# Rotary embedding on a Trainium2 core: block-exchanging copies in place of rotation products

## The chip, the cores and the metric

The kernel runs on one core of one Trainium2 chip. The metric is the device time of one execution in microseconds (us); three runs of the kernel before gave 915.8, 915.88 and 916.42, median 915.88. Engines are named as the profile names them: PE is TensorE (PEld its weight loads), DVE is VectorE, ACT is ScalarE, POOL is GpSimd, SP the queue that issues most of the loads.

## The reference, cut to what matters

Two transformer blocks run one after the other on 256 tokens of width 1024, in float32. The first has dilated attention, an RWKV-7 time mix and gates; the second three other attentions, gates, a memory and a feed-forward part. In both, queries and keys are rotated by position before they are used; both blocks' functions do the same:

```
half = HEAD_DIM // 2                       # heads of 64 columns
ang = pos[:, None] * inv_freq[None, :]
c, s = jnp.cos(ang), jnp.sin(ang)
x1, x2 = xf[..., :half], xf[..., half:]
return jnp.concatenate([x1 * c - x2 * s, x2 * c + x1 * s], axis=-1)
```

So a row of the first 32 of a head needs its partner 32 rows on, with a minus; a row of the second 32 its partner 32 rows back, with a plus.

## The kernel before, in words

Queries and keys are kept with features on the partitions and the 256 tokens in the free dimension, so a tile of 128 partitions holds two heads, each of two blocks of 32 rows. A projection is done in chunks of 256 features (`feature_chunk`): 8 slices of the model width, each as a product of the high part of the weights, one of their remainder (lines 807 and 808), and one of the high part with the activations' remainder (line 816), for two halves of 128 features, into one PSUM bank. The banks 0 and 1 take turns. The high part of a chunk's weights is copied by ScalarE (`split`, line 1820, in two halves), and VectorE subtracts it from the weights for the remainder (`split`, line 2703, in two halves); chunk n+1's split is done while TensorE works on chunk n, and TensorE's first products of a chunk wait for the first half's remainder.

Block one (tag "qk") has six chunks of first-block queries and keys, n = 0 to 5. Block two (tag "in2") has seven, of which n = 2 to 6 are rotated; n = 6 is 128 features wide, so its bank holds 256 columns and not 512. Behind it come two slots of value weights (464 columns wide), then the gates' slots (512 wide).

The steps of one rotated chunk before the change:

- ScalarE copies the bank to SBUF (`rope_read`, line 1985, recorded at the helper's line 1820) and so frees it in block two.
- TensorE multiplies the copy by a constant 128x128 matrix of ones and minus ones (`rotate`, line 766), in the middle of the next chunk's first half, into a bank of its own.
- The cosine product (copy or bank times cosine): in block one by VectorE from the chunk's bank (`cosines`, line 2809), after ScalarE's copy; in block two by GpSimd from the copy (`rope`, line 3698).
- The sine product by VectorE from the rotation's bank (line 2776).
- The sum of both: in block one by VectorE (line 2815), in block two by GpSimd (line 3703).

The order on each engine is written out by hand: each engine's program is a set of generators that are advanced in the same turns, and each engine takes its instructions strictly in that order. In block one the chunks ("m" turns) run beside the RWKV inverse ("s" turns; lines 1132, 1145, 1158, 1192 to 1225 on TensorE, lines 2957 to 2995 on VectorE, more copies at line 1820 on ScalarE); each of five levels of the inverse shares the time with one chunk. The inverse's banks (4 to 7) go round, and a product waits until the bank's last content was read: the one at line 1145 needs the banks of two transposed tiles (line 727), which ScalarE copies out. In block two ScalarE also makes three small copies of key rows (64x256) behind the last chunk.

Of the kernel before, what the change touches and what calls it, by code (L numbers as in the profile page):

```python
# [21 lines left out]

C_ID, C_SU, C_IU, C_LI, C_ONE, C_BLK, C_ROT, C_M0, C_D64 = [128 * i for i in range(9)]
C_LV = 128 * 9
C_MA = C_LV + 768
# [19 lines left out]
def shape_constants():  # L45
# [40 lines left out]
    c[0:64, C_SINC:C_SINC + 256] = np.tile(sin, (2, 1))  # L86
    return c
# [189 lines left out]
def program(nc, A, consts, vecs, pt, out):  # L277
    with ExitStack() as ctx:
# [55 lines left out]
        def const(off, n):  # L334
            return low[:, OC + off:OC + off + n]
# [236 lines left out]
        main_pe, main_act, main_dve, main_pool = [count("main_" + n) for n in ("pe", "act", "dve", "pool")]  # L572
        rope_pe, rope_act, rope_dve, rope_pool = [count("rope_" + n) for n in ("pe", "act", "dve", "pool")]
        rw_pe, rw_act, rw_dve, rw_pool = [count("rwkv_" + n) for n in ("pe", "act", "dve", "pool")]
# [133 lines left out]
        def tensor_program(e, turns):  # L708
# [42 lines left out]
            def seam(tag, i, at_once=False):  # L751
# [246 lines left out]
            def qkv():  # L998
                for s in range(3, 7):
                    yield from feature_chunk(st1, s, next(pg), plan_z[s][1], z_read(s), nothing)  # L1000
                yield from token_range(st1, V_AT, 2, 512, lambda i: [main_act.at("v", 0, i)], nothing)
                yield from token_range(st1, V_AT + 2, 1, 256, lambda i: [main_act.at("v", 1, i)], nothing)
                for n in range(6):
                    yield from feature_chunk(st1, QK_AT + n, next(pg), [128, 128], [rope_dve.at("qk", n, "cos")],
                                             (lambda n=n: rotate("qk", n - 1, 2, rz1[(n - 1) % 2])) if n else nothing)

# [3 lines left out]
            def gates():  # L1010
                for r in (2, 3, 0, 1):
                    yield from gate(r, (lambda: rotate("qk", 5, 2, rz1[1])) if r == 2 else nothing)

# [444 lines left out]

            def rotate2(n):
                if n >= 2:  # L1460
                    m = 1 if n == 6 else 2
                    rotate("in2", n, m, rz2[n % 2][:, 0:m, :])

            def read2(n):
                return [main_act.at("qa", n) if n < 2 else rope_act.at("in2", n)]

            turns.beside(head("in2", (0, 2), read2, lambda n: rotate2(n - 1)), seam("in2", 1, True), 3)

            def main_b():
                for n in range(2, 7):  # L1470
                    yield from feature_chunk(st2, n - 2, next(pg), plan_2[n][1], read2(n), lambda n=n: rotate2(n - 1))
                yield from token_range(st2, 5, 2, 464, lambda i: [main_act.at("vt2", i), main_dve.at("vt2", i)], lambda: rotate2(6))

# [333 lines left out]
        def scalar_program(e, turns):  # L1807
# [806 lines left out]
        def vector_program(e, turns):  # L2614
# [191 lines left out]

            def cosines(n, b):
                q.wait_ge(*rope_act.at("qk", n))
                tt(rt1[n % 2], halves(bank(b)), rep(const(C_COS, 256), 2), ALU.mult).then_inc(rope_dve.up("qk", n, "cos"), 1)

            def rotate1(n):
                dst = qk[:, 2 * n:2 * n + 2, :]
                rotate("qk", n, 2, dst, const(C_SIN, 256))
                q.wait_ge(*rope_dve.at("qk", n))
                tt(dst, dst, rt1[n % 2], ALU.add).then_inc(rope_dve.up("qk", n, "sum"), 1)

            def qkv():
# [5 lines left out]
                for n in range(6):  # L2823
                    b = next(pg)
                    yield from feature_chunk(st1, QK_AT + n, [128, 128], lambda: cosines(n, b), (lambda n=n: rotate1(n - 1)) if n else nothing)

# [463 lines left out]
            def rotate2(n):  # L3290
                if n >= 2:
                    rotate("in2", n, 1 if n == 6 else 2, rope_to(n), const(C_SINC if n == 6 else C_SIN, 256))

# [16 lines left out]
            def main_b():  # L3310
                for n in range(2, 7):
                    next(pg)
                    yield from feature_chunk(st2, n - 2, plan_2[n][1], nothing, lambda: rotate2(n - 1))
                yield from token_range(st2, 5, 2, read_vt, lambda: rotate2(6))
# [343 lines left out]
        def gpsimd_program(e, turns):  # L3658
# [36 lines left out]

            def rope(tag, n, m, zs, t1, cos):
                q.wait_ge(*rope_act.at(tag, n))
                tt(t1, zs, rep(cos, m), ALU.mult).then_inc(rope_pool.up(tag, n, "cos"), 1)

            def rotate(tag, n, dst, t1):  # L3700
                q.wait_ge(*rope_dve.at(tag, n))
                q.wait_ge(*rope_pool.at(tag, n, "cos"))
                tt(dst, dst, t1, ALU.add).then_inc(rope_pool.up(tag, n), 1)
# [121 lines left out]

            def first2(n):
                if n >= 2:
                    m = 1 if n == 6 else 2
                    rope("in2", n, m, rz2[n % 2][:, 0:m, :], rt2[n % 2][:, 0:m, :], const(C_COSC if n == 6 else C_COS, 256))
# [5 lines left out]
            turns.beside(head("in2", st2, first2, lambda n: second2(n - 1)), seam("in2", 1, True), 3)  # L3835

            def main_b():
                for n in range(2, 7):
                    yield from feature_chunk(st2, n - 2, plan_2[n][1], lambda: first2(n), lambda: second2(n - 1))
                yield from token_range(st2, 5, 2, lambda: second2(6))  # L3840
# [144 lines left out]
```

## Time and profile before

| | |
|---|---|
| three runs | 915.8, 915.88, 916.42 us |
| span of the profiled execution | 913.6 us |
| the runs' median beyond that span | 2.3 us (915.88 - 913.6) |
| TensorE busy | 892.5 us, 98% |
| VectorE busy | 606.5 us, 66% |
| ScalarE busy | 454.0 us, 50% |
| GpSimd busy | 43.3 us, 5% |
| the chain that ended last | TensorE 86%, VectorE 7%, ScalarE 3% |

The profile is of one execution; its page gives the span from the first to the last instruction and no time of its own beside it, so the runs' median is set against the span. A busy share counts an instruction from its start to its end, and neighbours on one engine overlap: where the text speaks of what an instruction costs, it uses the distance from one start to the next. In a timeline, an entry "x4" is four neighbours of one kind, and a bracket is the idle time before an instruction and what ended it.

### The profile page before, as it was taken

How to read it: one execution, taken by the hardware profiler on the slowest of the kernel's cores; microseconds unless marked ns; L12 is line 12 of the kernel's file. 1: busy time of each engine (PE TensorE's matmuls, PEld its weight loads, DVE VectorE, ACT ScalarE, POOL GpSimd, SP SyncE). 2: the span in 40 equal slices, each digit the busy share in tenths (PEclk: the TensorE clock that was granted, in tenths of full speed). 3: DMA queues.
4: the chain of work that ended last, by engine and by line, in shares of the span. 5: the costliest groups of instructions: out<-in, count | busy, mean ns of one | idle time of the engine just before them, and what ended most of it. 6: DMA issues, size and time to landing. Idle time of an engine off the chain costs nothing.

```text
span 913.6 us, 15401 instructions
## 1 busy us (share of the span) xinstructions
PE 892.5 (98%) x6552; PEld 753.8 (83%) x6552; DVE 606.5 (66%) x972; ACT 454.0 (50%) x731; POOL 43.3 (5%) x61
## 2 busy tenths in 40 slices
PE   7999999999899999999999999999999999999997
PEld 4999898787689888888889878776788788888885
DVE  4578978557856666656765577877863566666673
ACT  4775444436534444446444357473522545555561
POOL 0010000010000000000000440000000000000000
PEclk9999999999999999999999999999999999999999
DMA  9644333224578665555439664252717566665621
GB/s 338 187 139 139 102 102 116 60 91 137 187 252 280 187 189 194 202 192 185 135 96 237 151 230 142 94 185 96 263 55 208 138 185 186 191 192 194 201 96 47
DMA packets 131205, 150.78 MB, mean 165 GB/s; under 512 B 11808, under 2 KB 102176, under 8 KB 131008
## 3 DMA queue, kind: packets, MB, share of 16 engines
q1 hardware_dynamic: 129920, 145.57, 51.5%
q10 hardware_dynamic: 1216, 4.23, 1.2%
q8 instruction: 52, 0.85, 0.4%
q14 instruction: 17, 0.14, 0.1%
HBM read 148.73 MB, written 1.05 MB: 164 GB/s over the span
## 4 chain that ended last, share of the span: by engine, by line
PE 86%; DVE 7%; ACT 3%; issue 2%; DMA 1%; POOL 0%; POOLq 0%; ACTq 0%; DVEq 0%
PE psum L834 12%; PE psum L721 9%; PE psum L723 9%; PE psum L722 9%; PE psum L839 7%; PE psum L787 4%; PE psum L807 3%; PE psum L808 3%; PE psum L816 3%; PE psum L727 3%; PE psum L883 2%; PE psum L893 2%; PE psum L884 2%; DVE parts L2703 2%; PE psum L840 2%
## 5 line engine op out<-in xcount | busy, mean ns | idle before, releaser
L1820 ACT ACTIVATE parts<-low 128x1024 fp32r<-128x1024 f32 (+3 forms) x252 | 254.2, 1044 | 68.4 <-PE psum L723 50.2
L2703 DVE TENSOR_TENSOR parts<-low,parts 128x1024 fp32r<-128x1024 f32 (+3 forms) x156 | 186.9, 1228 | 28.5 <-ACT parts L1820 28.3
L721 PE MATMUL psum<-parts 128*128 128x512 f32 (+2 forms) x424 | 170.0, 401 | 1.8 <-DVE parts L2703 1.0
L723 PE MATMUL psum<-parts 128*128 128x512 f32 (+2 forms) x424 | 163.5, 386 | 0.0
L722 PE MATMUL psum<-parts 128*128 128x512 f32 (+2 forms) x424 | 163.4, 385 | 0.0
L1820 ACT ACTIVATE high<-psum 128x512 f32<-128x512 f32 (+4 forms) x95 | 52.4, 563 | 160.7 <-PE psum L840 76.4
L834 PE MATMUL psum<-parts 128*128 128x512 f32 x462 | 116.8, 392 | 0.0
L834 PEld LDWEIGHTS psum<-parts 128*128 128x128 f32 x462 | 86.9, 188 | 16.9
L721 PEld LDWEIGHTS psum<-parts 128*128 128x128 f32 x424 | 79.6, 188 | 23.1 <-issue 3.8
L723 PEld LDWEIGHTS psum<-parts 128*128 128x128 f32 x424 | 79.6, 188 | 16.3
L722 PEld LDWEIGHTS psum<-parts 128*128 128x128 f32 x424 | 79.8, 188 | 14.7 <-issue 0.7
L2768 DVE TENSOR_TENSOR parts<-low,parts 128x1024 fp32r<-128x1024 f32 x54 | 66.0, 1223 | 35.3 <-ACT parts L1820 35.3
L807 PE MATMUL psum<-parts 128*128 128x256 f32 (+2 forms) x312 | 82.4, 300 | 0.0
L808 PE MATMUL psum<-parts 128*128 128x256 f32 (+2 forms) x312 | 76.8, 282 | 0.0
L839 PEld LDWEIGHTS psum<-parts 128*128 128x128 f32 x528 | 72.0, 190 | 5.2
L839 PE MATMUL psum<-parts 128*128 128x256 f32 x528 | 73.6, 282 | 0.0
L807 PEld LDWEIGHTS psum<-parts 128*128 128x128 f32 (+2 forms) x312 | 58.8, 189 | 4.1 <-issue 3.2
L808 PEld LDWEIGHTS psum<-parts 128*128 128x128 f32 (+2 forms) x312 | 58.9, 189 | 2.3 <-issue 2.2
L3199 DVE TENSOR_TENSOR mid<-psum,high 128x512 f32<-128x512 f32 x33 | 22.8, 692 | 46.2 <-ACT high L1820 46.2
L816 PE MATMUL psum<-parts 128*128 128x256 f32 (+2 forms) x312 | 43.7, 283 | 0.0
L3666 POOL TENSOR_TENSOR low<-low 128x1 f32<-128x1 f32 x20 | 11.0, 550 | 635.6 <-DVE low L2624 319.4
L816 PEld LDWEIGHTS psum<-parts 128*128 128x128 f32 (+2 forms) x312 | 40.0, 189 | 0.1
(321 smaller groups left out, 1346.7 us busy)
## 6 DMA issues: line engine op xcount, KB each, us to landing
low<-in_w_in_dram SPq DMA_DIRECT2D x40, 1024.0 KB, 5.3
low<-in_w_ffn_in_dram SPq DMA_DIRECT2D x44, 512.0 KB, 5.2
low<-in_w_ff_in_dram SPq DMA_DIRECT2D x16, 1024.0 KB, 6.1
low<-in_w_ff_out_dram SPq DMA_DIRECT2D x16, 1024.0 KB, 4.9
low<-in_w_ffn_out_dram SPq DMA_DIRECT2D x11, 1024.0 KB, 5.0
low<-in_w_out_dram SPq DMA_DIRECT2D x8, 1024.0 KB, 5.2
low<-in_w_ple_gate_dram SPq DMA_DIRECT2D x4, 1024.0 KB, 5.2
low<-consts_dram ACTq DMA_DIRECT2D x1, 2142.0 KB, 9.2
```

The costliest lines, as they stand in the source:

```text
L721: mm(o, l[0], r[0], start, False)
L722: mm(o, l[0], r[1], False, False)
L723: return mm(o, l[1], r[0], False, stop)
L787: t = mm(PSUM[0:m, banks[n], 256 * j + 128 * i:256 * j + 128 * i + 128], w3[:, k, off:off + m], uT[:, k, 128 * i:128 * i + 128], k == 0, k ...
L807: mm(o, hi[:, k, c], st.uh[:, k, :], k == 0, False)
L808: mm(o, lo_[:, k, c], st.uh[:, k, :], False, False)
L816: t = mm(o, hi[:, k, c], st.ul[:, k, :], False, k == 7)
L834: mm(p, hi[:, k, c], st.u2(k), k == 0, False)
L839: mm(p[:, 0:256], lo_[:, k, c], st.uh[:, k, :], False, False)
L1820: return e.activation(o, a, ACT.Copy)
L2703: tt(rslot3(n, nk, width)[:, r, 0:w], slot3(n, nk, width)[:, r, 0:w], st.hi3(j)[:, r, 0:w].bitcast(F32), ALU.subtract) \
L2768: tt(rview(OR + 2048 * n + 1024 * (k % 2), 1024), slot(n)[:, 1024 * (k % 2):1024 * (k % 2) + 1024], rview(base, 1024).bitcast(F32), ALU.su ...
```

## The change

The rotation product is gone from TensorE, and its constant with it. ScalarE's one copy of a bank becomes four, each of 32 rows, each to the place of its neighbour block, so that the copy holds every row's partner. The minus stands in the table of sines now. The cosine product is VectorE's in both blocks, reads the bank, and comes first: ScalarE's copies wait for it. VectorE's sine product reads the exchanged copy in SBUF. A bank is free when ScalarE's copies are done. GpSimd keeps the sums of block two.

```diff
-    same = r // 64 == s // 64
-    c[:, C_ROT:C_ROT + 128] = (same & (r % 64 < 32) & (s % 64 == r % 64 + 32)) * 1.0 \
-        - (same & (r % 64 >= 32) & (s % 64 == r % 64 - 32)) * 1.0
...
-    c[:, C_SIN:C_SIN + 256] = np.tile(sin, (4, 1))
+    c[:, C_SIN:C_SIN + 256] = np.tile(np.concatenate([-sin, sin]), (2, 1))
...
-            def rotate(tag, n, m, z):
-
-                b = 2 + n % 2 if tag == "qk" else 5 + n % 3
-                p = bank(b)
-                q.wait_ge(*rope_act.at(tag, n))
-                mm(p[:, 0:256 * m], const(C_ROT, 128), z, True, True).then_inc(rope_pe.up(tag, n), 1)
-                free[b] = [rope_dve.at(tag, n)]
...
             def rope_read(tag, n, m, b, zs):
+
                 if n >= (2 if tag == "qk" else 4):
-                    q.wait_ge(*(rope_pe.at(tag, n - 2) if tag == "qk" else rope_pool.at(tag, n - 2)))
-                copy(zs, halves(bank(b))[:, 0:m, :]).then_inc(rope_act.up(tag, n), 1)
+                    q.wait_ge(*rope_dve.at(tag, n - 2))
+                q.wait_ge(*rope_dve.at(tag, n, "cos"))
+                z = halves(bank(b))
+                for p in range(4):
+                    t = copy(zs[32 * p:32 * p + 32, 0:m, :], z[32 * (p ^ 1):32 * (p ^ 1) + 32, 0:m, :])
+                t.then_inc(rope_act.up(tag, n), 1)
...
-            def rotate(tag, n, m, dst, sin):
-                q.wait_ge(*rope_pe.at(tag, n))
-                tt(dst, halves(bank(2 + n % 2 if tag == "qk" else 5 + n % 3))[:, 0:m, :], rep(sin, m), ALU.mult).then_inc(rope_dve.up(tag, n), 1)
+            def cosines(tag, n, m, b, t1, cos, made):
+                q.wait_ge(*made)
+                tt(t1, halves(bank(b))[:, 0:m, :], rep(cos, m), ALU.mult).then_inc(rope_dve.up(tag, n, "cos"), 1)
+
+            def rotate(tag, n, m, zs, dst, sin):
+
+                q.wait_ge(*rope_act.at(tag, n))
+                tt(dst, zs, rep(sin, m), ALU.mult).then_inc(rope_dve.up(tag, n), 1)
...
+            def cosines2(n, b):
+                m = 1 if n == 6 else 2
+                if n >= 4:
+                    q.wait_ge(*rope_pool.at("in2", n - 2))
+                cosines("in2", n, m, b, rt2[n % 2][:, 0:m, :], const(C_COSC if n == 6 else C_COS, 256), main_pe.at("st2", n - 2, 1))
...
-            def rope(tag, n, m, zs, t1, cos):
-                q.wait_ge(*rope_act.at(tag, n))
-                tt(t1, zs, rep(cos, m), ALU.mult).then_inc(rope_pool.up(tag, n, "cos"), 1)
```

How the instructions stand, with what each waits for. First ScalarE in block one, around the reads of chunks 0 and 1, before:

```order
L1820 ACTIVATE mid<-psum 128x512 [waits main_pe]
L1820 ACTIVATE parts<-low 128x1024 [waits slot_in0]
L1820 ACTIVATE high<-psum 128x512 [waits rwkv_pe,z_dve]
L1820 ACTIVATE parts<-low 128x1024
L1820 ACTIVATE high<-psum 128x512 [waits rwkv_pe]
L1820 ACTIVATE mid<-psum 128x512 [waits main_pe]
```

and now:

```order
L1803 ACTIVATE mid<-psum 32x512 [waits rope_dve,main_pe]
L1803 ACTIVATE mid<-psum 32x512 x3
L1803 ACTIVATE parts<-low 128x1024 [waits slot_in0]
L1803 ACTIVATE high<-psum 128x512 [waits rwkv_pe,z_dve]
L1803 ACTIVATE parts<-low 128x1024
L1803 ACTIVATE high<-psum 128x512 [waits rwkv_pe]
L1803 ACTIVATE mid<-psum 32x512 [waits rope_dve,main_pe]
L1803 ACTIVATE mid<-psum 32x512 x3
```

The places are the same; the read is four instructions (to "mid", the copy), and the first of them waits for VectorE's cosine product. The "high" copies are those of the two transposed tiles.

VectorE in block one at the same place, before:

```order
L2964 TENSOR_TENSOR high<-high,low 64x512
L2809 TENSOR_TENSOR mid<-psum,low 128x512 [waits rope_act]
L2776 TENSOR_TENSOR mid<-psum,low 128x512 [waits rope_pe]
L2815 TENSOR_TENSOR mid<-mid 128x512 [waits rope_dve]
L2703 TENSOR_TENSOR parts<-low,parts 128x1024 [waits split_act] x2
```

and now:

```order
L2955 TENSOR_TENSOR high<-high,low 64x512
L2764 TENSOR_TENSOR mid<-psum,low 128x512 [waits main_pe]
L2769 TENSOR_TENSOR mid<-mid,low 128x512 [waits rope_act]
L2804 TENSOR_TENSOR mid<-mid 128x512 [waits rope_dve]
L2691 TENSOR_TENSOR parts<-low,parts 128x1024 [waits split_act] x2
```

No instruction has moved; the cosine product (first of the three) waits for TensorE alone, and the sine product for ScalarE's copies.

VectorE in block two, chunks 2 to 4, before:

```order
L2703 TENSOR_TENSOR parts<-low,parts 128x1024 [waits split_act] x2
L2776 TENSOR_TENSOR high<-psum,low 128x512 [waits rope_pe]
...
L2703 TENSOR_TENSOR parts<-low,parts 128x4x128 [waits split_act] x2
L2776 TENSOR_TENSOR high<-psum,low 128x2x256 [waits rope_pe]
L2703 TENSOR_TENSOR parts<-low,parts 128x928 [waits split_act] x2
```

and now:

```order
L2691 TENSOR_TENSOR parts<-low,parts 128x1024 [waits split_act] x2
L2764 TENSOR_TENSOR high<-psum,low 128x512 [waits main_pe,rope_pool]
L2769 TENSOR_TENSOR high<-high,low 128x512 [waits rope_act]
L2691 TENSOR_TENSOR parts<-low,parts 128x4x128 [waits split_act] x2
L2764 TENSOR_TENSOR high<-psum,low 128x512 [waits main_pe,rope_pool]
L2769 TENSOR_TENSOR high<-high,low 128x2x256 [waits rope_act]
L2691 TENSOR_TENSOR parts<-low,parts 128x928 [waits split_act] x2
```

Between the two remainders of the next weights and the sine product stands a cosine product now, of the chunk that TensorE has just ended.

## Rows read from the trace of the kernel before

**Rows 1.** The page, busy time of each engine and instructions.
```profile
PE 892.5 (98%) x6552; PEld 753.8 (83%) x6552; DVE 606.5 (66%) x972; ACT 454.0 (50%) x731; POOL 43.3 (5%) x61
```

**Rows 2.** Line 766, the rotations: count, duration in ns, first and last start.
```profile
L766 PE MATMUL psum<-mid,low x12: 590/590/594, 94.2 to 147.9; 128*128 128x512 f32 x12
...
L766 PE MATMUL psum<-high,low x10: 378/590/594, 502.4 to 526.7; 128*128 128x512 f32 x8, 128*128 128x256 f32 x2
```

**Rows 3.** TensorE's timeline in block one: start, duration, what, idle before.
```profile
94.24 1.02 PE L766 MATMUL psum<-mid,low 128*128 128x512 f32 x2
95.10 0.60 PE L727 MATMUL psum<-low,high 128*128 128x128 f32 x4
...
101.46 1.16 PE L1145 MATMUL psum<-high 64*128 64x128 f32 x16
...
107.80 0.24 PE L1217 MATMUL psum<-mid,high 64*64 64x64 f32 x1 [0.16 <-DVE high L2971]
```

**Rows 4.** VectorE's timeline in block one.
```profile
90.54 0.45 DVE L2957 COPY_PREDICATED high<-low,psum 128x256 f32<-128x256 int32 x1 [0.98 <-PE psum L1132]
...
98.69 0.69 DVE L2809 TENSOR_TENSOR mid<-psum,low 128x512 f32<-128x512 f32 x1
99.30 0.68 DVE L2776 TENSOR_TENSOR mid<-psum,low 128x512 f32<-128x512 f32 x1
100.02 0.69 DVE L2815 TENSOR_TENSOR mid<-mid 128x512 f32<-128x512 f32 x1
...
118.70 2.35 DVE L2703 TENSOR_TENSOR parts<-low,parts 128x1024 fp32r<-128x1024 f32 x2
123.85 0.69 DVE L2809 TENSOR_TENSOR mid<-psum,low 128x512 f32<-128x512 f32 x1 [2.80 <-ACT mid L1820]
```

**Rows 5.** ScalarE's timeline in block one.
```profile
93.00 0.60 ACT L1820 ACTIVATE mid<-psum 128x512 f32<-128x512 f32 x1 [4.53 <-PE psum L816]
...
112.06 0.60 ACT L1820 ACTIVATE mid<-psum 128x512 f32<-128x512 f32 x1 [1.97 <-PE psum L816]
112.56 2.00 ACT L1820 ACTIVATE parts<-low 128x1024 fp32r<-128x1024 f32 x2
...
123.22 0.60 ACT L1820 ACTIVATE mid<-psum 128x512 f32<-128x512 f32 x1 [1.92 <-PE psum L816]
```

**Rows 6.** ScalarE's timeline in block two.
```profile
501.19 0.60 ACT L1820 ACTIVATE high<-psum 128x512 f32<-128x512 f32 x1 [3.27 <-PE psum L816]
...
507.81 0.60 ACT L1820 ACTIVATE high<-psum 128x512 f32<-128x512 f32 x1 [1.51 <-PE psum L816]
...
524.74 0.38 ACT L1820 ACTIVATE high<-psum 128x256 f32<-128x256 f32 x1 [1.39 <-PE psum L816]
526.22 1.30 ACT L1820 ACTIVATE high<-high 64x256 f32<-64x256 f32 x3 [1.09 <-POOL high L3703]
```

**Rows 7.** TensorE's timeline behind block two's chunks.
```profile
525.10 0.47 PE L721 MATMUL psum<-parts 128*128 128x464 f32 x1 [0.39 <-DVE parts L2703]
...
535.97 0.37 PE L723 MATMUL psum<-parts 128*128 128x464 f32 x1
536.18 0.40 PE L721 MATMUL psum<-parts 128*128 128x512 f32 x1
```

**Rows 8.** ScalarE's timeline behind block one: copies of 64 rows.
```profile
152.73 0.59 ACT L1820 ACTIVATE high<-psum 64x512 f32<-64x512 f32 x1
153.23 0.58 ACT L1820 ACTIVATE mid<-psum 64x512 f32<-64x512 f32 x1
153.83 0.59 ACT L1820 ACTIVATE high<-psum 64x512 f32<-64x512 f32 x1
```

**Rows 9.** GpSimd's and VectorE's timelines in block two.
```profile
504.27 1.30 POOL L3703 TENSOR_TENSOR high<-high 128x512 f32<-128x512 f32 x1 [1.11 <-DVE high L2776]
510.88 2.21 POOL L3703 TENSOR_TENSOR high<-high 128x512 f32<-128x512 f32 x1 [1.11 <-DVE high L2776]
...
511.85 2.32 DVE L2703 TENSOR_TENSOR parts<-low,parts 128x1024 fp32r<-128x1024 f32 x1
```

More of the change, by code:

```diff
@@ L20 @@
 S0 = math.exp(-0.5)
-C_ID, C_SU, C_IU, C_LI, C_ONE, C_BLK, C_ROT, C_M0, C_D64 = [128 * i for i in range(9)]
-C_LV = 128 * 9
+C_ID, C_SU, C_IU, C_LI, C_ONE, C_BLK, C_M0, C_D64 = [128 * i for i in range(8)]
+C_LV = 128 * 8
 C_MA = C_LV + 768
@@ L572, in program @@
         main_pe, main_act, main_dve, main_pool = [count("main_" + n) for n in ("pe", "act", "dve", "pool")]
-        rope_pe, rope_act, rope_dve, rope_pool = [count("rope_" + n) for n in ("pe", "act", "dve", "pool")]
+        rope_act, rope_dve, rope_pool = [count("rope_" + n) for n in ("act", "dve", "pool")]
         rw_pe, rw_act, rw_dve, rw_pool = [count("rwkv_" + n) for n in ("pe", "act", "dve", "pool")]
@@ L1003, in qkv @@
                 for n in range(6):
-                    yield from feature_chunk(st1, QK_AT + n, next(pg), [128, 128], [rope_dve.at("qk", n, "cos")],
-                                             (lambda n=n: rotate("qk", n - 1, 2, rz1[(n - 1) % 2])) if n else nothing)
+                    yield from feature_chunk(st1, QK_AT + n, next(pg), [128, 128], [rope_act.at("qk", n)], nothing)
             def gate(r, late):
@@ L1011, in gates @@
                 for r in (2, 3, 0, 1):
-                    yield from gate(r, (lambda: rotate("qk", 5, 2, rz1[1])) if r == 2 else nothing)
+                    yield from gate(r, nothing)
             rw_bank = itertools.cycle((4, 5, 6, 7))
@@ L1457, in tensor_program @@
             st2 = ST["st2"]
[L1459 to L1462, printed above, removed]
             def read2(n):
                 return [main_act.at("qa", n) if n < 2 else rope_act.at("in2", n)]
-            turns.beside(head("in2", (0, 2), read2, lambda n: rotate2(n - 1)), seam("in2", 1, True), 3)
+            turns.beside(head("in2", (0, 2), read2, nothing), seam("in2", 1, True), 3)
             def main_b():
                 for n in range(2, 7):
-                    yield from feature_chunk(st2, n - 2, next(pg), plan_2[n][1], read2(n), lambda n=n: rotate2(n - 1))
-                yield from token_range(st2, 5, 2, 464, lambda i: [main_act.at("vt2", i), main_dve.at("vt2", i)], lambda: rotate2(6))
+                    yield from feature_chunk(st2, n - 2, next(pg), plan_2[n][1], read2(n), nothing)
+                yield from token_range(st2, 5, 2, 464, lambda i: [main_act.at("vt2", i), main_dve.at("vt2", i)], nothing)
             turns.alone(main_b())
@@ L2804, in vector_program @@
             e.tensor_copy(identb, ident).then_inc(init_dve.up("idb"), 1)
-            def cosines(n, b):
-                q.wait_ge(*rope_act.at("qk", n))
-                tt(rt1[n % 2], halves(bank(b)), rep(const(C_COS, 256), 2), ALU.mult).then_inc(rope_dve.up("qk", n, "cos"), 1)
             def rotate1(n):
                 dst = qk[:, 2 * n:2 * n + 2, :]
-                rotate("qk", n, 2, dst, const(C_SIN, 256))
+                rotate("qk", n, 2, rz1[n % 2], dst, const(C_SIN, 256))
                 q.wait_ge(*rope_dve.at("qk", n))
@@ L2824, in qkv @@
                     b = next(pg)
-                    yield from feature_chunk(st1, QK_AT + n, [128, 128], lambda: cosines(n, b), (lambda n=n: rotate1(n - 1)) if n else nothing)
+                    yield from feature_chunk(st1, QK_AT + n, [128, 128],
+                                             lambda: cosines("qk", n, 2, b, rt1[n % 2], const(C_COS, 256), main_pe.at("st1", QK_AT + n, 1)),
+                                             (lambda n=n: rotate1(n - 1)) if n else nothing)
             def gate(r, late):
@@ L3291, in rotate2 @@
                 if n >= 2:
[L3292 removed]
+                    m = 1 if n == 6 else 2
+                    rotate("in2", n, m, rz2[n % 2][:, 0:m, :], rope_to(n), const(C_SINC if n == 6 else C_SIN, 256))
+            def cosines2(n, b):
+                m = 1 if n == 6 else 2
+                if n >= 4:
+                    q.wait_ge(*rope_pool.at("in2", n - 2))
+                cosines("in2", n, m, b, rt2[n % 2][:, 0:m, :], const(C_COSC if n == 6 else C_COS, 256), main_pe.at("st2", n - 2, 1))
             turns.beside(head("in2", st2, nothing, lambda n: rotate2(n - 1)), seam_ple(1), 3)
@@ L3311, in main_b @@
                 for n in range(2, 7):
-                    next(pg)
-                    yield from feature_chunk(st2, n - 2, plan_2[n][1], nothing, lambda: rotate2(n - 1))
+                    b = next(pg)
+                    yield from feature_chunk(st2, n - 2, plan_2[n][1], lambda: cosines2(n, b), lambda: rotate2(n - 1))
                 yield from token_range(st2, 5, 2, read_vt, lambda: rotate2(6))
@@ L3833, in second2 @@
                     rotate("in2", n, rope_to(n), rt2[n % 2][:, 0:1 if n == 6 else 2, :])
-            turns.beside(head("in2", st2, first2, lambda n: second2(n - 1)), seam("in2", 1, True), 3)
+            turns.beside(head("in2", st2, nothing, lambda n: second2(n - 1)), seam("in2", 1, True), 3)
             def main_b():
                 for n in range(2, 7):
-                    yield from feature_chunk(st2, n - 2, plan_2[n][1], lambda: first2(n), lambda: second2(n - 1))
+                    yield from feature_chunk(st2, n - 2, plan_2[n][1], nothing, lambda: second2(n - 1))
                 yield from token_range(st2, 5, 2, lambda: second2(6))
```

7 lines of the change are left out of this document (1 added, 6 removed).

## The prediction, made before the changed kernel had run

> **What bounds the kernel now.** I read the busy shares first: TensorE is busy 98% of the span [rows 1]. Its timeline has almost no gap around the rotations, so TensorE's time is nearly all on the path; the question is what each removed product frees, and whether something else then comes late. Next I read the rotation's own line: eleven products, each two passes [rows 2]. Last come the timelines of TensorE, VectorE and ScalarE through the two stretches with rotary work. I call them block one (six chunks, 88 to 150 us) and block two (five chunks, 495 to 530 us).
>
> In block one VectorE is behind. It works without a break from 90.54 until its product at line 2971 lets TensorE go on at 107.80, after a gap of 0.16 us [rows 3, 4]. ScalarE's copy of chunk 0 ran at 93.00, but VectorE's cosine product of the same chunk only at 98.69 [rows 4, 5]: 5.7 us apart, which cost nothing because the copy did not wait for it. From 112 us on a level (one chunk, one step of the inverse) takes 11.16 us (ScalarE's reads at 112.06 and 123.22 [rows 5]), TensorE has no gap, and VectorE idles 2.80 us of it [rows 4]. In block two a chunk takes 6.61 us (501.19 to 507.81 [rows 6]); VectorE idles there, and TensorE waits only at the end, 0.39 us at 525.10 [rows 7].
>
> **What goes.** The rotation at 94.24 is followed by the next product at 95.10 [rows 3], so one costs 0.86 us; the eleventh, 256 columns wide, half of it. Together 10 x 0.86 + 0.43 = 9.0 us of a gapless TensorE. GpSimd loses its cosine products; VectorE gets them in block two, five of up to 0.69 us (the cosine product of rows 4). VectorE's sine product reads SBUF where it read PSUM; the product that read PSUM took 0.68 at 99.30 and the sum of two SBUF tensors 0.69 at 100.02 [rows 4], so I cost that at nothing.
>
> **What comes: the copies.** One copy of 128x512 was a single instruction. Now four of 32x512 exchange the blocks. The narrow copies are no shorter: 0.58 to 0.59 us for 64 rows [rows 8], as for 128. What counts is when the next starts. The copies at 152.73 and 153.23 write the same half of the partitions (lines 2125 and 2126) and are 0.50 apart; the next goes to the other half and starts 0.60 later [rows 8]. Every exchanging copy changes its block, so I take 0.61 x 4 = 2.43 us; the bounds are 0.50 x 4 = 2.0 and, at worst, the same again plus a handoff for each (2.6). The Trainium skill, "VectorE: DVE Perf Modes", section "Two Vector instructions with no wait between them", says that an instruction whose operand starts in another group of 32 partitions than the one before is held until all earlier ones finish, and says it of VectorE alone. Read strictly, ScalarE would copy at 0.50, and the sum would be that of the second rival.
>
> **Block one.** ScalarE's first copy now waits for the cosine product that ends at 98.69 + 0.69 = 99.38, and 2.43 later, at 101.85, VectorE's sine product may start; before it started at 99.30 [rows 4]. VectorE was the path, so everything to 107.80 moves by 2.6. ScalarE's two weight halves and its copies of two transposed tiles queue behind these copies: 101.85 + 2.0 (the pair at 112.56 [rows 5]) + 2 x 0.5 = 104.9. TensorE's product at 101.46 [rows 3] needs those tiles' banks, and waits some 4 us. From there to 107.64 it took 6.2, now 5.3 without a rotation: 104.9 + 5.3 = 110.2, just before 107.80 + 2.6 = 110.4, so the two delays do not add. Rotations 0 and 1 are swallowed in this; 2 to 5 free 4 x 0.86 = 3.44. In a later level the copies end 3.15 after a chunk's end (0.69 + 2.43 and handoffs), and VectorE takes its sine product only 5.3 after it, behind seven others, so nothing new waits: a level of 10.30 still covers VectorE's 8.4 (11.16 - 2.80). Block one: +2.6 - 3.44 = **-0.85 us**; bounds -5.2 (copies hidden) and +2 (another such stall).
>
> **Block two.** Here the new order closes a loop through three engines. VectorE runs, per chunk: sine product, two weight remainders, cosine product of the next chunk. That cosine product releases ScalarE's copies, they release the sine product, and GpSimd's sum follows the sine product. The sum and VectorE's remainders exclude each other: a sum alone takes 1.30 [rows 9], but the one issued at 510.88, right after VectorE had begun a remainder, took 2.21, and VectorE's second remainder (issued 511.85) took 2.32 instead of half of the pair's 2.35 [rows 4, 9]. So one sum costs VectorE some 1.2. In the new order the remainder has to wait for ScalarE's half, 1.0 to 1.05 after the copies [rows 5], while the sum starts 0.83 after them; the sum goes first. (The Trainium skill, "SBUF — State Buffer", "SBUF: two separate sides", calls this an exclusive lock held for a whole instruction, which is how rows 9 read; by its word the price would be 1.3 and the sum below 0.4 us more.)
>
> One turn of the loop: cosine 0.69, copies 2.43, sine 0.69, sum 1.2, two remainders 2.3, three handoffs 0.05 to 0.08 each: **7.45 us**. TensorE alone would need 6.61 - 0.86 = 5.75, and had 6.61 before. Walked through: cosine products start at 501.2, 508.65 and 516.1, then 522.6 (the fourth slot is half as wide: 6.5). The last copies end 3.2 later at 525.8, sine 526.55, sum until 527.8, first remainder of the next weights at 529.0. TensorE, ready at about 525, starts there, where it started at 525.10 before [rows 7]: +3.9. Then the short chunk: cosine from 530.0, four copies of 256 columns (0.38 each) until 532.0, the three key copies 1.3 [rows 6], ScalarE's half 1.0, VectorE's remainder 1.15: TensorE gets the second slot at 535.45, and needs 24 x 0.21 = 5.05 for it [rows 7]. It ends at 540.5; before, the gates began at 536.18 [rows 7]. Block two: **+4.3 us**. Bounds: -3.9 (all five rotations freed) and +5.3 (each group of copies 0.2 dearer).
>
> **The sum**: -0.85 + 4.3 = +3.5. The profiled execution spans 913.6 us, so this is a span of 917.1; the runs' times stand 2.3 above that span (median 915.88). I predict 919.3 us. No later stage takes it back: behind 540 every engine waits for TensorE again.
>
> **Rivals.** (1) *The sum does not hold VectorE* where it now stands, since it starts before the remainder is issued. The loop is then 6.6 in block two, the cosine products come at 507.8, 514.4 and 519.5, and the second slot at 531.2, against 531.1 before: no change there, 915.1 in all. Against: what the collision in rows 9 cost VectorE (1.2) is a sum alone (1.30) to 0.1 us. (2) *Copies follow each other at 0.50*: -1.25 in block one, and a loop of 7.0, +1.9 in block two, 916.5. Against: 0.60 in rows 8. (3) *Faster*: both are cheap. The loop falls below 6.6, the point from which it decides, to about 6.1; TensorE reaches the gates 1.9 early, with -1.25 from block one 912.7. If nothing waited at all, 906.9. For it: TensorE is the only engine that is full. (4) *Worse*: the stall of block one is repeated in a later level, or the copies cost 0.65; 921 to 922.
>
> **How the numbers follow.** What a measurement of this kernel can tell from no change is about 0.2%, 1.8 us. The forecast has 0.55, rival 1 and rival 2 together 0.25 (both within 0.2%), rival 3 0.14, rival 4 0.06. Slower: 0.61; same: 0.25; faster: 0.14. The range goes from rival 1 with a little to spare, 914.6, to the edge of rival 4, 921.5; rival 3 and the far tail are left out.
>
> **What would show it.** In the profile after: the copies of 32 rows about 0.61 apart; in block one a wait of TensorE of about 4 us near 100 to 105, on ScalarE, and levels of 10.3 us after it; in block two chunks of about 7.4 us, with TensorE waiting for VectorE's remainders before each, longest before the 464-wide slot, and sums of 1.3 us with a remainder of 1.2 behind each. Wrong if chunks of block two last 6.0 us or less, or if TensorE's wait near 100 us is under 2 us.

## The result and the profile after

| | before | after |
|---|---|---|
| median of four runs each | 915.9 us (915.8 to 916.42) | 923.75 us (922.82 to 924.3) |
| ratio, 95% interval | | 1.0084 (1.0072 to 1.0097) |
| the profiled execution: span | 913.6 us | 922.0 us |
| its mean granted clock of TensorE | 0.998 | 0.992 |

The kernel is slower by 7.9 us where 3.4 were forecast, and outside the range (914.6 to 921.5). The page of the changed kernel has, for its first line, what answers to [rows 1]; the second is the granted clock in 40 slices of 23 us, in tenths of full speed:

```profile
PE 890.6 (97%) x6530; PEld 755.5 (82%) x6530; DVE 610.1 (66%) x977; ACT 473.6 (51%) x764; POOL 34.1 (4%) x56
...
PEclk9999899999999999999999989999999999999999
```

TensorE has 22 instructions fewer, the two passes of each of the eleven rotations, but its busy time fell by only 1.9 us, where they had held it for 9.0. Two slices of PEclk hold an 8: the fifth (92 to 115 us, block one) and the 24th (530 to 553 us, the end of block two). Instructions that run slower fill the busy time that the rotations left.

TensorE's timeline shows where it waited. Of block one all waits from 0.2 us up are here; the last three lines stand before chunks of block two and before the first product of the value weights. These answer to [rows 3] and [rows 7]:

```profile
105.13 2.08 PE L1133 MATMUL psum<-high 64*128 64x128 f32 x16 [4.49 <-ACT high L1803]
124.21 0.21 PE L1205 MATMUL psum<-mid,high 64*64 64x64 f32 x1 [0.28 <-issue]
144.29 0.24 PE L1205 MATMUL psum<-mid,high 64*64 64x64 f32 x1 [0.20 <-DVE mid L2976]
145.07 0.21 PE L1206 MATMUL psum<-high 64*64 64x64 f32 x1 [0.25 <-issue]
...
511.06 0.36 PE L796 MATMUL psum<-parts 128*128 128x256 f32 x1 [0.79 <-DVE parts L2691]
518.45 0.35 PE L796 MATMUL psum<-parts 128*128 128x256 f32 x1 [1.31 <-DVE parts L2691]
531.89 0.73 PE L718 MATMUL psum<-parts 128*128 128x464 f32 x1 [4.06 <-DVE parts L2691]
```

The waits are where the prediction put them, and nearly as long. What it did not have is what follows them. In the view by windows (columns: window, length, then busy us and count of PE, PEld, DVE, ACT, POOL, then PEclk, DMA share, GB/s) the granted clock is 1.00 ahead of each of the two long waits and 0.50, the lower of the two levels (1.2 in place of 2.4 GHz), for some six microseconds behind it:

```profile
96.00:100.00 4.00, 4.00 (x64) 3.87 (x65) 3.25 (x5) 0.53 (x1) 0.00 (x0) 1.00 0.43 151
105.00:111.00 6.00, 5.87 (x34) 5.67 (x35) 5.88 (x9) 4.36 (x6) 0.00 (x0) 0.50 0.01 3
112.00:118.00 6.00, 6.00 (x213) 5.80 (x216) 2.72 (x3) 2.09 (x5) 0.00 (x0) 1.00 0.01 3
526.00:530.00 4.00, 1.83 (x16) 1.63 (x14) 1.18 (x3) 3.63 (x6) 0.50 (x1) 1.00 1.05 245
532.00:537.00 5.00, 5.00 (x13) 4.37 (x14) 1.53 (x3) 3.65 (x9) 1.73 (x5) 0.50 0.67 270
539.00:545.00 6.00, 6.00 (x30) 5.36 (x29) 4.17 (x10) 2.47 (x4) 2.30 (x10) 1.00 0.55 175
```

A busy share hides it: in 105 to 111 us TensorE is busy 98% of the time, but the sixteen products at line 1133 (line 1145 before) take 2.08 us where they took 1.16 [rows 3]. The product at 531.89 takes 0.73 us where its like took 0.47 [rows 7]. The Trainium skill, "TensorE: Matmul & The Clock Gate", Part 1, says that idleness puts the array at half clock, sustained work brings it back, and that it looks at the activity on a grid of its own that no kernel starts; this trace agrees with the first two (0.50 from within the wait of 4.49 us, 1.00 again after six microseconds of work), and no run here shows the third.

The copies are as priced. ScalarE's timeline answers to [rows 5, 6], a group of four at 0.60 us each and its distance to the next instruction 2.41:

```profile
99.47 2.38 ACT L1803 ACTIVATE mid<-psum 32x512 f32<-32x512 f32 x4 [11.02 <-DVE mid L2764]
101.88 1.06 ACT L1803 ACTIVATE parts<-low 128x1024 fp32r<-128x1024 f32 x1
102.96 0.60 ACT L1803 ACTIVATE high<-psum 128x512 f32<-128x512 f32 x1
103.45 1.05 ACT L1803 ACTIVATE parts<-low 128x1024 fp32r<-128x1024 f32 x1
104.40 0.59 ACT L1803 ACTIVATE high<-psum 128x512 f32<-128x512 f32 x1
```

The queue that the prediction counted off (copies, two halves, two tiles) ends at 104.99; it had said 104.9. VectorE's timeline of block one answers to [rows 4]: the cosine product at the same 98.69, then 2.51 us of idleness, and the cosine products of chunks 2 to 5, whose distances are the levels, 10.82, 10.40 and 10.68 us:

```profile
98.69 0.69 DVE L2764 TENSOR_TENSOR mid<-psum,low 128x512 f32<-128x512 f32 x1
101.89 0.69 DVE L2769 TENSOR_TENSOR mid<-mid,low 128x512 f32<-128x512 f32 x1 [2.51 <-ACT mid L1803]
...
117.19 0.69 DVE L2764 TENSOR_TENSOR mid<-psum,low 128x512 f32<-128x512 f32 x1 [3.16 <-PE psum L805]
128.01 0.69 DVE L2764 TENSOR_TENSOR mid<-psum,low 128x512 f32<-128x512 f32 x1 [1.99 <-PE psum L805]
138.41 0.69 DVE L2764 TENSOR_TENSOR mid<-psum,low 128x512 f32<-128x512 f32 x1 [1.56 <-PE psum L805]
149.09 0.69 DVE L2764 TENSOR_TENSOR mid<-psum,low 128x512 f32<-128x512 f32 x1 [1.23 <-PE psum L805]
```

One turn of the loop in block two, from VectorE's and GpSimd's timelines (the sum, third line, answers to [rows 9]):

```profile
507.76 0.69 DVE L2769 TENSOR_TENSOR high<-high,low 128x512 f32<-128x512 f32 x1 [2.51 <-ACT high L1803]
508.84 3.20 DVE L2691 TENSOR_TENSOR parts<-low,parts 128x1024 fp32r<-128x1024 f32 x2 [0.39 <-ACT parts L1803]
...
508.53 1.30 POOL L3696 TENSOR_TENSOR high<-high 128x512 f32<-128x512 f32 x1 [19.21 <-DVE high L2769]
...
511.97 0.68 DVE L2764 TENSOR_TENSOR high<-psum,low 128x512 f32<-128x512 f32 x1
515.16 0.69 DVE L2769 TENSOR_TENSOR high<-high,low 128x512 f32<-128x512 f32 x1 [2.51 <-ACT high L1803]
```

The turn is 7.40 us (507.76 to 515.16), forecast 7.45. The pair of remainders took 3.20 us in place of 2.35, because the sum had begun 0.31 before it.

Two marks tell how much each block costs, in every kernel below. The first is ScalarE's copy of 512 columns between the two halves at the start of block two: 498.80 us here, 495.43 before, so **block one costs +3.4**. The second is TensorE's first wait of 0.4 us behind block two: 579.02 here, 570.38 before, 8.64 later, so **block two costs +5.3**. At the end it is 8.4. The lines are, of the change and of the kernel before in turn:

```profile
498.80 0.60 ACT L1803 ACTIVATE high<-psum 128x512 f32<-128x512 f32 x1 [1.08 <-PE psum L776]
495.43 0.60 ACT L1820 ACTIVATE high<-psum 128x512 f32<-128x512 f32 x1 [1.08 <-PE psum L787]
...
579.02 0.50 PE L718 MATMUL psum<-parts 128*128 128x512 f32 x1 [0.40 <-DVE parts L2691]
570.38 0.50 PE L721 MATMUL psum<-parts 128*128 128x512 f32 x1 [0.40 <-DVE parts L2703]
```

### The profile page after: what moved, and what is told of

It reads as the page before. It is cut to its first block, busy times and chain, and to the rows that moved or that the text cites. A ratio compares the mean times of both kernels' runs of the same rounds, so it can differ in the third digit from the quotient of the medians.

```text
span 922.0 us, 15393 instructions
## 1 busy us (share of the span) xinstructions
PE 890.6 (97%) x6530; PEld 755.5 (82%) x6530; DVE 610.1 (66%) x977; ACT 473.6 (51%) x764; POOL 34.1 (4%) x56
## 4 chain that ended last, share of the span: by engine, by line
PE 85%; DVE 6%; ACT 4%; issue 2%; DMA 1%; POOL 0%; POOLq 0%; ACTq 0%; DVEq 0%
PE psum L823 12%; PE psum L718 10%; PE psum L720 9%; PE psum L719 9%; PE psum L828 7%; PE psum L776 4%; PE psum L796 3%; PE psum L797 3%; PE psum L805 3%; PE psum L724 3%; PE psum L872 2%; PE psum L882 2%; PE psum L873 2%; DVE parts L2691 2%; PE psum L829 2%
## 5 line engine op out<-in xcount | busy, mean ns | idle before, releaser
L1803 ACT ACTIVATE high<-psum 128x512 f32<-128x512 f32 (+7 forms) x110 | 60.5, 560 | 142.7 <-PE psum L829 76.4
L796 PEld LDWEIGHTS psum<-parts 128*128 128x128 f32 (+2 forms) x312 | 59.9, 192 | 5.2 <-issue 3.9
L797 PEld LDWEIGHTS psum<-parts 128*128 128x128 f32 (+2 forms) x312 | 60.1, 193 | 0.3 <-issue 0.3
L1803 ACT ACTIVATE mid<-psum 32x512 f32<-32x512 f32 (+7 forms) x55 | 29.3, 547 | 42.4 <-DVE mid L2764 23.5
L805 PEld LDWEIGHTS psum<-parts 128*128 128x128 f32 (+2 forms) x312 | 40.4, 191 | 0.0
```

What stands on the lines that cost most here:

```text
L796: mm(o, hi[:, k, c], st.uh[:, k, :], k == 0, False)
L797: mm(o, lo_[:, k, c], st.uh[:, k, :], False, False)
L805: t = mm(o, hi[:, k, c], st.ul[:, k, :], False, k == 7)
L1803: return e.activation(o, a, ACT.Copy)
```

## The experiments

### Does the clock explain what is missing? (three kernels)

In place of idling, TensorE does products whose result nobody reads: five ahead of the products at line 1133 in block one, four ahead of the value weights in block two.

```diff
+                    if i == 0:
+                        for _ in range(5):
+                            mm(bank(2), const(C_BLK, 128), const(0, 512), True, True)
...
+                for _ in range(4):
+                    mm(bank(5), const(C_BLK, 128), const(0, 512), True, True)
                 yield from token_range(st2, 5, 2, 464, ...)
```

The five alone:

> The changed kernel with five extra 128x512 products of constants on TensorE (0.86 us each, 4.3 in all, into a bank nobody reads) just ahead of the product that waits 4.49 us for ScalarE in block one. They lie in that wait. Theory C (the granted clock): TensorE no longer falls to 1.2 GHz from 104.7 to 111.1 us; the level behind is about 2.9 us shorter, the median about 920.8. Rival Q (queues alone set the time; what is behind the wait is bound by VectorE anyway): no change, 923.7.

Measured: 921.83 us (920.65 to 922.01), ratio to before 1.0061 (1.0048 to 1.0073).

The four alone:

> The changed kernel with four such extra products (3.4 us) ahead of the value weights in block two, where TensorE waits 4.06 us for VectorE's remainder. Theory C: the stretch at 1.2 GHz from 531 to 537 us is gone; TensorE then reaches the second slot of value weights early and waits some 1.3 us for its remainder, so about 1.5 us come back: 922.3. Rival Q: 923.7, or above it by what the extra products delay.

Measured: 922.78 us (921.57 to 923.18), ratio 1.0072 (1.0059 to 1.0084).

Both:

> Both fillings. Theory C: the two gains add, about 919.3. Rival Q: 923.7.

Measured: 919.78 us (919.42 to 921.34), ratio 1.0046 (1.0032 to 1.0059). The windows of the kernel with both have the clock at 1.00 where it was 0.50, and 122 products from 105 to 111 us where there were 34; the last line is the cosine product of chunk 2, which stood at 117.19:

```profile
105.00:111.00 6.00, 5.87 (x122) 5.25 (x125) 5.88 (x9) 4.47 (x7) 0.00 (x0) 1.00 0.02 3
112.00:118.00 6.00, 6.00 (x104) 5.42 (x104) 4.75 (x6) 3.31 (x7) 0.00 (x0) 1.00 0.30 83
...
532.00:537.00 5.00, 4.20 (x20) 3.44 (x19) 3.10 (x4) 4.65 (x7) 4.82 (x9) 1.00 0.33 90
...
114.97 0.69 DVE L2769 TENSOR_TENSOR mid<-psum,low 128x512 f32<-128x512 f32 x1 [0.81 <-PE psum L805]
```

Nine products that compute nothing make the kernel 4.0 us faster (923.75 - 919.78). That is the gap between 923.75 and the forecast of 919.3, but for 0.5. Alone they gave 1.9 and 1.0 where 2.9 and 1.5 were expected; the interval of the four alone (1.0059 to 1.0084) overlaps that of the change (1.0072 to 1.0097), so of the medians it is the kernel with both that decides against queues alone. By the marks: block one falls from +3.4 to +0.3 with both fills and to +1.1 with the first alone, which is the same code up to there; the 0.8 between them lies in the levels, not in the stall (one profiled execution of each). Block two falls from +5.3 to +4.0. Half a microsecond of work is lost per microsecond at 0.50, some 3 us from 531 us on, but only 1.3 of it was on the path: with the clock up TensorE reaches the second slot too early and waits there, the 0.80 us that the slow clock had swallowed (the prediction's times leave 535.45 - 529.0 - 5.05 = 1.4 there):

```profile
528.79 0.45 PE L718 MATMUL psum<-parts 128*128 128x464 f32 x1 [0.62 <-DVE parts L2696]
...
535.28 0.48 PE L718 MATMUL psum<-parts 128*128 128x464 f32 x1 [0.80 <-DVE parts L2696]
```

### Block one without its stall

For chunk 0 alone the old order stays: ScalarE copies as soon as the chunk is there, and VectorE's cosine product comes behind the copies and frees the bank.

```diff
-                q.wait_ge(*rope_dve.at(tag, n, "cos"))
+                if (tag, n) != ("qk", 0):
+                    q.wait_ge(*rope_dve.at(tag, n, "cos"))
...
-                ... main_pe.at("st1", QK_AT + n, 1)),
+                ... main_pe.at("st1", QK_AT + n, 1) if n else rope_act.at("qk", 0)),
```

> The changed kernel, but for chunk 0 of block one alone ScalarE copies first (as soon as the chunk is done, near 93 us) and VectorE's cosine product waits for the copies. Theory (one stall in block one, made by that one wait, with the clock behind it): VectorE's chain to 107.8 us is as before, TensorE never waits 4.5 us and keeps its clock; block one goes from 3.3 us longer than before the change to 2.4 to 3.4 shorter: median 917.0 to 918.2. Rival Q (without a share of the clock): only the 2.6 us by which VectorE's chain moved come back, 921.1. Rival: each of the later levels stalls too, so one chunk alone gives a sixth.

Measured: 918.29 us (917.73 to 918.87), ratio 1.0026 (1.0016 to 1.0035), 5.5 us less than the change. TensorE's timeline of block one has no wait of 4 us, and the clock stays at 1.00 through it; the wait ahead of the value weights is the same:

```profile
101.98 0.36 PE L796 MATMUL psum<-parts 128*128 128x256 f32 x1 [0.25 <-DVE parts L2692]
106.47 0.24 PE L1205 MATMUL psum<-high 64*64 64x64 f32 x1 [1.28 <-DVE high L2987]
...
526.65 0.45 PE L718 MATMUL psum<-parts 128*128 128x464 f32 x1 [4.06 <-DVE parts L2692]
```

Block one is now -1.9: the removed rotations do pay there, as soon as one wait is in the right place. 5.5 us is more than the 2.6 by which VectorE's chain had moved, so queues alone don't account for it. VectorE's sine product starts at 99.29, as it did before (99.30 [rows 4]).

### Which part makes the loop of block two?

**Sums on VectorE.** GpSimd's five sums of block two go to VectorE, right behind the sine product (`tt(rope_to(n), rope_to(n), rt2[n % 2], ALU.add)`).

> The changed kernel with the sums of block two on VectorE (0.7 us each) and not on GpSimd. Theory (GpSimd's sum keeps VectorE's remainder waiting 1.1 to 1.2 us): the loop falls from 7.41 to about 7.0, 1.5 us in block two, and 3 more if TensorE's wait ahead of the value weights gets short enough to keep the clock: 922.2 or 919.3. Rival (the two do not exclude each other, the remainder was late for another reason): the loop grows by the sum's 0.7 to 8.1 us, 926.

Measured: 920.77 us (920.21 to 920.87), ratio 1.0055 (1.0042 to 1.0067), 3.0 less than the change. VectorE's timeline:

```profile
508.16 0.69 DVE L3286 TENSOR_TENSOR high<-high 128x512 f32<-128x512 f32 x1
508.77 2.35 DVE L2691 TENSOR_TENSOR parts<-low,parts 128x1024 fp32r<-128x1024 f32 x2
511.04 0.68 DVE L2764 TENSOR_TENSOR high<-psum,low 128x512 f32<-128x512 f32 x1
...
517.85 0.69 DVE L2764 TENSOR_TENSOR high<-psum,low 128x512 f32<-128x512 f32 x1
```

The loop is 6.81 us (511.04 to 517.85) in place of 7.40, although VectorE has one operation more in it: the pair of remainders is back at 2.35. A sum given to another engine cost more here than one done in place. Block two is +1.9. And TensorE's wait ahead of the value weights is 3.07 us, but in the profiled execution the clock did not fall behind it. That execution is the fastest of the five (920.21 us, mean clock 0.996); the other four have 920.69 to 920.87 us at 0.993 to 0.995, so the clock may have fallen there. The window behind the wait, in the profiled one:

```profile
529.00:532.00 3.00, 2.60 (x12) 2.17 (x12) 1.63 (x3) 1.25 (x4) 0.00 (x0) 1.00 1.04 369
```

**One copy in place of four.** The 32-row blocks are not exchanged, so the rotation is left out of the result; all else stands.

```diff
-                for p in range(4):
-                    t = copy(zs[32 * p:32 * p + 32, 0:m, :], z[32 * (p ^ 1):32 * (p ^ 1) + 32, 0:m, :])
+                t = copy(zs, z[:, 0:m, :])
```

> The changed kernel with one copy of 128 rows in place of the four of 32, with the same waits; the blocks are not exchanged, so the rotation is left out of the result. It prices the four copies. Theory: the loop of block two falls by 1.9 to 5.5 us, under TensorE's 5.75; in block one TensorE's wait falls from 4.5 to about 2.3 us, VectorE's chain moves by 0.65 and not 2.6. About 911. Rival (the wait for the cosine product is the cost, not the copies): chunks of block two stay above 6.5 and block one's wait above 4 us, 920 or above. Whether a wait of 2.3 us lowers the clock is open: with it 3 us more.

Measured: 912.83 us (912.07 to 914.75), ratio 0.9973 (0.9964 to 0.9983). The cosine products of block two start at 501.59, 507.46, 513.18 and 518.94, so a chunk takes 5.7 to 5.9 us, TensorE's own pace (5.75 in the prediction). So the 1.65 us that the loop takes beyond that come from the three extra copies, which are 1.8 us per chunk, and not from the wait for the cosine product; block two without them is a gain, -1.3. In block one TensorE's wait is 2.42 us in place of 4.49. Of the ten executions seven lie at 912.1 to 913.0 with a mean clock of 0.996 to 0.999, and three at 914.72 to 914.75 with 0.995. The profiled one is of these three, and its clock fell behind a wait of only 1.82 us:

```profile
523.53 0.45 PE L718 MATMUL psum<-parts 128*128 128x464 f32 x1 [1.82 <-DVE parts L2690]
...
524.00:527.00 3.00, 3.00 (x9) 2.60 (x9) 1.18 (x3) 2.05 (x5) 1.23 (x3) 0.50 1.02 365
```

### Another order in block two

The first attempt moves ScalarE's copies behind the next slot's halves, and VectorE's sine product behind the two remainders, so that the weights that TensorE waits for come first.

```diff
                     if n < 2:
                         split(st, j + 1, (n,))
+                    if n == 1 and pending:
+                        pending.pop()()
...
-                    yield from feature_chunk(..., lambda: read2(n, b))
+                    yield from feature_chunk(..., lambda: pending.append(reads))
...
-                    ... lambda: cosines2(n, b), lambda: rotate2(n - 1))
+                    ... lambda: (rotate2(n - 1), cosines2(n, b)), nothing)
```

> The changed kernel with another order in block two: ScalarE takes the halves of the next weights before a chunk's four copies, and VectorE the two remainders before the sine product. Theory (the loop of cosine, copies, sine, sum and remainders, 7.4 us a turn, is what block two costs): the loop is open, chunks last about 5.75 us, TensorE no longer waits 4 us ahead of the value weights nor loses its clock. Block two goes from 5.3 us longer than before the change to about 3.5 shorter: median 915.0. Rival (ScalarE's or VectorE's own work in a chunk is what binds): chunks of 6.5 us or more, 919 or above.

Measured: 920.31 us (918.77 to 922.55), ratio 1.0052 (1.0038 to 1.0066). Together with the order of block one from above:

> Both reorderings together (chunk 0 of block one copies first; block two's copies and sine products behind the weights). The first alone gave 918.3. If the two costs are separate they add: 918.3 - 8.8 = 909.5, some 6 us below the kernel before the change. If block two's chunks cannot go under 6.5 us, 914 or above.

Measured: 915.76 us (914.62 to 916.82), ratio 1.0000 (0.9991 to 1.0009). Both stay some 5 or 6 us above what was expected of them: in the first, the cosine products of block two start at 504.71, 512.97, 520.00 and 525.76, so the loop is open, but of the distances only the last is TensorE's pace, 5.76 us. ScalarE's timeline of the first of the two says why:

```profile
507.90 2.01 ACT L1803 ACTIVATE parts<-low 128x1024 fp32r<-128x1024 f32 x2 [6.45 <-DMA low<-in_w_in_dram]
509.94 2.39 ACT L1803 ACTIVATE high<-psum 32x512 f32<-32x512 f32 x4
```

and TensorE's the consequence:

```profile
512.38 0.39 PE L796 MATMUL psum<-parts 128*128 128x256 f32 x1 [1.95 <-ACT high L1803]
...
530.02 0.48 PE L718 MATMUL psum<-parts 128*128 128x464 f32 x1 [1.48 <-ACT high L1803]
...
534.72 0.48 PE L718 MATMUL psum<-parts 128*128 128x464 f32 x1 [1.91 <-ACT high L1803]
```

The slot's transfer had not landed before 507.9, so the halves waited 6.45 us and the copies behind them too, with the bank that TensorE needed next. In the change the copies had run in just this time (505.34 to 507.73). The two later waits are for banks as well: the value weights were to go to those that the last two chunks are copied from. Behind the wait of 1.95 the clock fell once more (0.50 from 514 to 517 us).

So two repairs were tried on the version with both orders: the first chunk's copies ahead of the halves again (`reads() if n == 2 else pending.append(reads)`),

> As the version with both orders changed (915.76 us), but in block two the first chunk's four exchanging copies stand ahead of ScalarE's halves of the next slot again. In that version the halves wait until 502.7 us for their transfer, the copies behind them end at 507.1, and TensorE waits 1.72 us for their bank. Theory (the copies belong where ScalarE waits for a transfer anyway): that wait goes but for 0.2 us, and the time is 915.76 - 1.5 = 914.3 us. Rival (block two then goes by the transfers, so that what is gained at its start is waited for at the value weights): within 0.5 us of 915.8.

measured: 913.33 us (912.9 to 915.71), ratio 0.9979 (0.9970 to 0.9989); and with it the value weights in two free banks (`banks = [5, 6]`),

> The same, and the value weights' products go to two banks that nothing is reading (numbers 5 and 6) in place of the two that the last rotations are copied from. In the version before it TensorE waits 1.48 and 1.94 us there, both for ScalarE's copies. Theory (a copy that is late holds its bank, and the bank holds TensorE): the waits are then for the remainders, 0.3 and 0.7 us, and the time is 914.3 - 2.4 = 911.9 us. Rival (the transfer of the slot, which ScalarE waits 1.3 us for at 526.1 us, sets the second of them): 0.4 us less than the version above at most 1.2 us, so 913.1 or more. If it were banks alone that cost block two its time, the gain would be the whole 3.4 us: 910.9.

measured: 912.68 us (911.91 to 912.94), ratio 0.9963 (0.9950 to 0.9975). The first gave 2.4 where 1.5 were expected: the wait of 1.72 us went, and with it a fall of the clock (0.50 from 508 to 510 us in the version before). Six of its ten executions lie at 912.9 to 913.4 us and four at 914.75 to 915.71. The second gave 0.65, less than these intervals tell apart and near its rival's 0.4 to 1.2 rather than the theory's 2.4: the two bank waits are gone, but the transfers set the pace a little later, as TensorE's timeline behind the value weights and ScalarE's show:

```profile
532.57 0.50 PE L718 MATMUL psum<-parts 128*128 128x512 f32 x1 [1.14 <-DVE parts L2705]
...
531.75 2.01 ACT L1805 ACTIVATE parts<-low 128x1024 fp32r<-128x1024 f32 x2 [1.19 <-DMA low<-in_w_in_dram]
```

It is 3.2 us faster than the kernel before and 11 us faster than the change, with as many instructions as the change on TensorE, VectorE, ScalarE and GpSimd (6530, 977, 764 and 56). The free banks could be given to the kernel before too, but it waits only 0.39 us [rows 7] and 0.17 us at these places.

### All by the two marks

The marks are those of the one profiled execution of each kernel, the last column is the median of all its executions. The profiled execution was 1.6 us slower than the median for the one with copies and sine late, 1.9 for the one with one copy, 0.9 for "the same, chunk 0 in the old order".

| kernel | block one, us | block two, us | median, us |
|---|---|---|---|
| the change | +3.4 | +5.3 | 923.75 |
| fill in block one | +1.1 | +5.2 | 921.83 |
| fill in block two | +3.4 | +4.0 | 922.78 |
| both fills | +0.3 | +4.0 | 919.78 |
| chunk 0 in the old order | -1.9 | +4.1 | 918.29 |
| sums on VectorE | +3.0 | +1.9 | 920.77 |
| copies and sine late | +3.5 | +2.7 | 920.31 |
| the same, chunk 0 in the old order | -1.4 | +2.5 | 915.76 |
| and first copies ahead of the halves | -1.9 | -0.6 | 913.33 |
| and free banks | -1.8 | -1.2 | 912.68 |
| one copy for four | +0.4 | -1.3 | 912.83 |

## Why the prediction was wrong

The sign and the places were right, the size was not: a span of 922.0 against 917.1, 4.9 us more. Point by point.

- **Copies, "0.61 x 4 = 2.43".** Right: 2.38 for a group and 2.41 to the next instruction. The Trainium skill's rule of the change of partition group ("VectorE: DVE Perf Modes", "Two Vector instructions with no wait between them"), which it states of VectorE, describes ScalarE here too; rival 2 was wrong.
- **Block one, "everything moves by 2.6" and "waits some 4 us".** The wait was 4.49 us and ended at 105.13 (forecast 104.9). With the clock held up by the fills, the cosine product of chunk 2 stands at 114.97, 2.9 later than the read at 112.06 [rows 5]: 0.3 more than forecast. **The step that failed is what comes behind it**, "from there to 107.64 it took 6.2, now 5.3": that work was priced at full clock. It takes 5.3 us with the fills (105.26 to 110.58) and 7.9 in the changed kernel (105.13 to 112.99), where the cosine product of chunk 2 stands at 117.19: the clock costs **2.2 us**.
- **Block one, "2 to 5 free 4 x 0.86 = 3.44".** With the fills 2.65 came back (+2.9 at the mark, +0.3 at the end); levels are 10.32 us, as forecast 10.30, but the last one before was 10.57 and not 11.16 ([rows 5] show only the first two starts), so there was less to free: **0.8 us**. In the changed kernel three levels take 31.90 in place of 30.95, with waits of 0.28, 0.20 and 0.25, two of them "issue": **0.95 us** more. This is the rule and the 30.95 the exception: in the profiled executions of the other nine kernels the three levels take 31.4 to 32.4, so 3.44 was too much to count on. Together block one: 0.3 + 2.2 + 0.8 + 0.95 = 4.2, which is +3.4 against -0.85.
- **Block two, the loop of 7.45.** Right: 7.42 and 7.40. The sum holds VectorE where it now stands, so rival 1 was wrong: from the end of the sine product to the end of the remainders it is 3.59 us (508.45 to 512.04), forecast 3.5. With the fills block two costs +4.0, forecast +4.3.
- **Block two, the first product of the value weights.** It waited 4.06 us, and **the same step failed**: the forecast has the 24 products of the first slot done when the second slot's weights come, which at 0.21 each they are. At half clock they take 7.9 us (531.89 to 539.77) in place of 5.3, and the second slot starts late. The clock took 1.3 us of the path there.
- **Range and rivals.** Rival 4 (921 to 922) had the right side for another reason, a stall repeated. No rival had the clock, although the forecast itself put two waits of some 4 us into a trace in which the longest from 60 to 520 us was 1.51, and in which the clock was at 1.00 throughout.

The sum: 4.2 in block one, 1.0 in block two, and 0.3 less after them: 4.9 us. By cause: the clock 3.5; less freed in the levels 1.75; the rest nearly cancels (+0.3, -0.3 and -0.3). What stays open is the 0.95 in the levels: the two fills share all code of block one and still differ by 0.8 there, so it is not the stall. In the second and third level the products of 128x256 take the same 6.13 us in the kernel with both fills and in the slower ones; the difference lies between products of 64x64. No run told what makes the "issue" waits there.

## What to carry to other kernels

A wait put into a busy TensorE costs its length and then, behind 11 of the 16 waits of more than 1.7 us that the profiles hold, a stretch at half clock: look at the granted clock in the windows behind every wait of more than a microsecond or two, and price the products there at both levels. When a copy is made to wait for something, list what is queued behind it, whose bank it holds, and whether its engine would have been waiting for a transfer anyway: one wait in the right order was worth 5.5 us here, where all the rotations together had held TensorE for 9.0. An operation moved to an idle engine isn't free if it excludes the busy one; five sums done by VectorE itself were 3.0 us cheaper than by GpSimd.

## What the runs showed that was not expected

The length of a wait alone does not tell whether the clock falls. From the profiled executions, the longer waits of the two blocks with the clock behind each, and one from elsewhere:

| wait of TensorE, us | kernel | granted clock behind it |
|---|---|---|
| 4.49 or 4.48 | the change, block one; so in three more that share its block one | 0.50 for nearly 7 us in all four |
| 4.06 | the change, block two; 4.05 with the fill in block one | 0.50 for nearly 7 us in both |
| 4.06 | chunk 0 in the old order, block two | 0.50 for over 3 us |
| 3.07 | sums on VectorE | stays 1.00 |
| 2.42 | one copy for four, block one | 0.50 for over 3 us |
| 1.95 | copies and sine late | 0.50 for over 3 us |
| 1.94, 1.48 | the same, chunk 0 in the old order; 1.91, 1.48 without that order; 1.92, 1.48 with the first copies ahead | stays 1.00 in all three |
| 1.73 | copies and sine late, chunk 0 in the old order, at 231.64 us | stays 1.00 |
| 1.82 | one copy for four, block two | 0.50 for over 3 us |
| 1.72 | copies and sine late, chunk 0 in the old order | 0.50 for over 3 us |
| 1.28 | chunk 0 in the old order, block one | stays 1.00 |

A fall cost 1.7 or 3.4 us of TensorE's work (half of the time at 0.50), and which of the two came was not the wait's doing alone either: both stand behind a wait of 4.06. The waits of 1.72 and 1.73 are of one execution. That one kernel falls in some executions and not in others is inferred from their mean clocks, as only one of each was profiled: it would be the spread of the version with one copy, 912.1 to 914.75, where twenty executions of the kernel before, whose longest wait from 60 to 520 us is 1.51, lie at 915.1 to 916.9. The grid of which the Trainium skill tells ("TensorE: Matmul & The Clock Gate", Part 1), and which no kernel sets, would make such differences; no run here shows the grid.
